# The first two units of a diffusion backbone on scaled, unnormalised x, with the scale groups of the modulation loaded ahead of the shift groups

## The chip, the cores and the metric

The kernel runs on one core of a Trainium2 chip. The metric is the device time of one execution in microseconds (us); lower is better. The engines are TensorE (PE in the profile, with PEld for its weight loads), VectorE (DVE), ScalarE (ACT), GpSimd (POOL) and SyncE (SP), which here only issues transfers. An engine's name with a q (SPq, ACTq) is its queue of issues.

## The reference

Two layers of a diffusion backbone run over 256 latent tokens x and 256 context tokens, each a row of 1024 channels. Each layer has a half-step SwiGLU feed-forward network (FFN), a token mixer and a second FFN. Only the first FFN of the first layer and what it begins with matter here. For each of two streams (tokens modulated by c, context by c_ctx):

```python
m = split(silu(c) @ mod_w[l] + mod_b[l], 9)      # m[0] shift, m[1] scale, m[2] gate of the first FFN
u = rms_norm(x, norm_ffn1[l]) * (1 + m[1]) + m[0]
a, g = split(u @ w_in, 2)
x = x + 0.5 * m[2] * ((silu(g) * a) @ w_out)
```

rms_norm divides each token by the root of its mean square over the 1024 channels (plus 1e-6) and multiplies by a gain per channel. The root is one number per token, so it may be applied behind the matmul: with A = gain * (1 + scale), u @ w is rstd * ((x * A) @ w) + shift @ w.

## The kernel before, in words

**Layout.** Activations lie channels on partitions: `x`, `u_hi` and `u_lo` have 8 chunks (DC) of 128 channels by 512 tokens (256 latent, 256 context). Products keep fp32 precision by splitting both sides in a rounded part and a rest (`w_hi`, `w_lo`, `u_hi`, `u_lo`); `three` (L1112 to L1115) issues three matmuls of 512 columns per chunk. A weight tile is 8 chunks of 128 x 128, 512 KB, in a ring of four. SP loads `w_raw` (L313) once POOL is through with the tile four before; ACT rounds it into `w_hi` (L434), POOL subtracts into `w_lo` (L402), PE may then use it. A hidden unit of the FFN takes two tiles, j = 0 (value) and j = 1 (gate). `pair` (L1117) runs both tiles of a unit chunk by chunk, so that it can follow the making of u; units 0 and 1 go through it, later ones through `products`.

**Modulation.** `mod_w` is read in groups of 512 columns, 2 MB each. Groups 0 and 1 hold the shifts of the first norm, 2 and 3 its scales; within each kind the first group serves chunks 0 to 3 and the second chunks 4 to 7. `mod_rounds` (L1183) runs 16 matmuls for a group into bank 6, ACT copies it (`copy_mod`, L505), `mod_turn` (L1191) transposes it into bank 7, and DVE reduces it into columns (`mod_extract`, L829). Four groups (N_START) are loaded by SP into `mod_first` (L317), in the order of `START_GROUPS`; the later ones come by ACT's queue (`load_mod`, L499), one or two transfers ahead of use.

**The start.** SP issues, in this order: identity, vectors, x, ctx, groups 0 and 2, the two tiles of unit 0, groups 1 and 3, then the tiles of unit 1 and all further ones. PE transposes the token rows chunk by chunk (`turn_x`, L1253), DVE copies each chunk to `x` (L934), ACT squares it (L449) and DVE adds the squares up (L768). PE sums over channels (`mean_square`, L1163), ACT takes the root (L464), DVE the reciprocal and a diagonal matrix (L783, L784), and `spread` (L1170) puts rstd on all partitions of bank 5. After groups 0 and 2 are through, DVE forms `colB` (shift) and `colA` (gain times 1 + scale) for chunks 0 to 3 (`columns_norm`, L747 to L749).

**A norm.** In `norm`, DVE makes `tmp` = x * colA * rstd (L799), ACT `u_hi` = tmp + colB, rounded (L488), DVE `u_lo` the rest (L812), each in two halves by stream. In the start it does chunks 0 to 3, then groups 1 and 3 are taken in (`start_columns(1)`), then chunks 4 to 7. PE has these two groups between its fourth and fifth chunk of unit 0, and group 4 between units 0 and 1.

**Later norms.** For k > 0 the first pair doesn't wait for the norm. ACT's `first_scaled` (L456) and DVE's `first_split` (L775) make u_hi and u_lo of x * colA without rstd and shift; PE's first pair uses them, with `mean_square` and `spread` among its chunks, and follows with 32 matmuls of 4 columns that multiply the weights with the shifts (L1153, L1154, from `shift_split`). ACT and DVE then overwrite u with the normalised one for all other units, and `first_hidden` (L868) applies rstd and shift to unit 0's products. ACT's part of the norm begins with w_hi of the tiles 2 and 3 and has those of 4 and 5 ahead of chunks 5 and 7.

From unit 2 on all runs in a loop (`turns`), the same in every sub-layer. DVE and ACT wait for each other and for PE by semaphores; `link` makes DVE wait for its own instruction.

## Time and profile before

| what | value |
|---|---|
| median of 3 runs | 2162.15 us (2160.63 to 2166.5) |
| the profiled execution, its own time | 2160.53 us |
| its span, first to last instruction | 2158.7 us |
| mean granted clock of TensorE | 0.984 |
| busy: PE / DVE / ACT / POOL | 96% / 39% / 31% / 44% |
| chain that ended last | PE 81%, issue 8%, DVE 5%, POOL 4% |

The page is one profiled execution. A busy share is the time in which an engine has at least one instruction under way; the matmuls are pipelined, so a mean duration of one is longer than the distance to the next. The chain follows the work that ended last back from the end. Time on it is time of the kernel; idle time of an engine off the chain costs nothing. The granted clock is a share of 2.4 GHz, 0.5 being 1.2 GHz. In the timeline an entry gives start, duration, engine, line, operation, out<-in and, in brackets, how long the engine had been idle and who released it.

### The profile page before, as it was taken

The numbers are of one execution on the slowest core, as the hardware profiler recorded it, in microseconds if no ns is written. First come the engines' busy times: TensorE is split into PE (matmuls) and PEld (weight loads), VectorE is DVE, ScalarE is ACT, GpSimd is POOL, SyncE is SP. The second block draws the span as 40 slices with busy tenths as digits, with TensorE's granted clock in tenths as the row PEclk, the third lists the DMA queues.
The fourth block names the chain that finished last, engine by engine and source line by source line (L and its number), as shares of the span: only waits on it lengthen the run. The fifth ranks groups of instructions, "written<-read, shape, count | busy, mean of one in ns | idle before, by whom it ended". The sixth has DMA issues, their size and how long they took to land.

```text
span 2158.7 us, 30089 instructions
## 1 busy us (share of the span) xinstructions
PE 2081.9 (96%) x10694; PEld 1675.0 (78%) x10694; DVE 849.6 (39%) x1320; ACT 670.0 (31%) x1057; POOL 940.7 (44%) x424
## 2 busy tenths in 40 slices
PE   4899999999999999999999999999999899989998
PEld 2677777887557888877877787787778766989998
DVE  4333123356472213623132454322333836573313
ACT  3221222243343223422222242222224333444333
POOL 2244434343102444444444444444434321876886
PEclk8999999999999999999999999999999899999999
DMA  8555654244101333454455236534624420654564
GB/s 280 167 164 154 218 163 150 81 112 105 48 1 49 97 90 95 122 171 143 120 156 169 67 105 202 155 100 138 192 75 112 125 69 16 180 157 137 170 187 127
DMA packets 445425, 278.98 MB, mean 129 GB/s; under 512 B 33906, under 2 KB 407148, under 8 KB 445356
## 3 DMA queue, kind: packets, MB, share of 16 engines
q1 hardware_dynamic: 401868, 206.79, 33.6%
q10 hardware_dynamic: 43360, 71.05, 10.0%
q8 instruction: 42, 0.69, 0.1%
q0 software_dynamic: 128, 0.23, 0.0%
q14 instruction: 27, 0.22, 0.0%
HBM read 276.98 MB, written 1.05 MB: 129 GB/s over the span
## 4 chain that ended last, share of the span: by engine, by line
PE 81%; issue 8%; DVE 5%; POOL 4%; SPq 1%; ACT 1%; DMA 1%; POOLq 0%; DVEq 0%; ACTq 0%
PE bank L1113 24%; PE bank L1115 24%; PE bank L1114 24%; POOL w_lo L402 4%; PE bank L1183 3%; PE bank L1392 1%; PE bank L1340 1%; DVE u_lo L812 1%; PE bank L1376 1%; PE bank L1191 1%; DVE tmp L799 1%; SPq L313 1%; DMA w_raw<-in_ffn_w_in 1%; DVE rstd L971 1%; SPq L317 1%
## 5 line engine op out<-in xcount | busy, mean ns | idle before, releaser
L402 POOL TENSOR_TENSOR w_lo<-w_raw,w_hi 128x1024 fp32r<-128x1024 f32 (+2 forms) x412 | 937.5, 2292 | 1205.4 <-ACT w_hi L434 1205.3
L1113 PE MATMUL bank<-u_hi,w_hi 128*128 128x512 f32 (+1 forms) x2016 | 742.2, 368 | 22.8 <-DVE u_lo L812 20.7
L1114 PE MATMUL bank<-u_lo,w_hi 128*128 128x512 f32 (+1 forms) x2016 | 728.2, 361 | 0.0
L1115 PE MATMUL bank<-u_hi,w_lo 128*128 128x512 f32 (+1 forms) x2016 | 727.6, 361 | 0.0
L1113 PEld LDWEIGHTS bank<-u_hi,w_hi 128*128 128x128 f32 x2016 | 387.5, 192 | 105.0 <-issue 28.0
L434 ACT ACTIVATE w_hi<-w_raw 128x1024 fp32r<-128x1024 f32 (+2 forms) x412 | 385.6, 969 | 177.3 <-PE bank L1115 167.2
L1115 PEld LDWEIGHTS bank<-u_hi,w_lo 128*128 128x128 f32 x2016 | 386.8, 192 | 57.5
L1114 PEld LDWEIGHTS bank<-u_lo,w_hi 128*128 128x128 f32 x2016 | 387.6, 192 | 56.0 <-issue 1.7
L857 DVE TENSOR_TENSOR hf<-bank,sg 128x512 f32<-128x512 f32 (+1 forms) x85 | 53.2, 626 | 586.5 <-ACT sg L529 586.5
L1113 PE MATMUL bank<-h_hi,w_hi 128*128 128x512 f32 (+1 forms) x704 | 258.2, 367 | 3.9 <-DVE x L841 3.2
L1115 PE MATMUL bank<-h_hi,w_lo 128*128 128x512 f32 (+1 forms) x704 | 256.1, 364 | 0.0
L1114 PE MATMUL bank<-h_lo,w_hi 128*128 128x512 f32 (+1 forms) x704 | 254.3, 361 | 0.0
L529 ACT ACTIVATE sg<-bank 128x512 f32<-128x512 f32 (+1 forms) x85 | 46.4, 546 | 655.4 <-PE bank L1115 655.4
L865 DVE TENSOR_TENSOR h_lo<-hf,h_hi 128x512 f32 (+3 forms) x88 | 177.8, 2020 | 9.4
L841 DVE SCALAR_TENSOR_TENSOR x<-bank,colG,x 128x256 f32 (+1 forms) x136 | 60.5, 480 | 279.6 <-PE bank L1115 277.8
L1113 PEld LDWEIGHTS bank<-h_hi,w_hi 128*128 128x128 f32 x704 | 132.3, 188 | 27.9 <-issue 6.3
L1115 PEld LDWEIGHTS bank<-h_hi,w_lo 128*128 128x128 f32 x704 | 132.2, 188 | 23.0
L1114 PEld LDWEIGHTS bank<-h_lo,w_hi 128*128 128x128 f32 x704 | 132.1, 188 | 21.9
L1064 DVE TENSOR_TENSOR tmp<-bank,sig 128x512 f32<-128x512 f32 (+1 forms) x48 | 23.8, 552 | 182.1 <-PE bank L1115 182.1
L449 ACT ACTIVATE sq<-x 128x512 f32<-128x512 f32 (+3 forms) x56 | 32.0, 571 | 194.1 <-DVE x L841 184.2
L687 ACT ACTIVATE sig<-bank 128x512 f32<-128x512 f32 (+1 forms) x48 | 23.7, 493 | 180.2 <-PE bank L1115 180.2
L1183 PE MATMUL bank<-mod_w,sil 128*32 128x512 f32 x512 | 61.6, 598 | 0.0
(146 smaller groups left out, 1667.5 us busy)
## 6 DMA issues: line engine op xcount, KB each, us to landing
w_raw<-in_ffn_w_in SPq DMA_DIRECT2D x176, 512.0 KB, 3.9
mod_w<-in_mod_w ACTq DMA_DIRECT2D x64, 1024.0 KB, 7.3
w_raw<-in_w_in SPq DMA_DIRECT2D x68, 512.0 KB, 3.8
w_raw<-in_ffn_w_out SPq DMA_DIRECT2D x64, 384.0 KB, 3.4
w_raw<-in_ffn_w_out SPq DMA_DIRECT2D x64, 320.0 KB, 3.3
mod_first<-in_mod_w SPq DMA_DIRECT2D x4, 2048.0 KB, 14.9
w_raw<-in_w_o SPq DMA_DIRECT2D x16, 512.0 KB, 4.0
w_raw<-in_w_in SPq DMA_DIRECT2D x16, 256.0 KB, 4.3
```

The source lines that it names most:

```text
L402: pool.tensor_tensor(w_lo[:, slot, 0:n, :], w_raw[:, slot, 0:n, :], w_hi[:, slot, 0:n, :].bitcast(F32), ALU.subtract).then_inc(S("w_lo_rea ...
L434: act.activation(w_hi[:, slot, 0:n, :], w_raw[:, slot, 0:n, :], ACT.Copy).then_inc(S("w_hi_ready"), 1)
L449: act.activation(sq[:, par, 0:n], x[:, bass.ds(m, 1), 0:n].rearrange("p a n -> p (a n)"), ACT.Square).then_inc(S("sq_ready"), 1)
L529: act.activation(sg[:, b, 0:n], bank[:, 2 * b + 1, 0:n], ACT.Silu).then_inc(S("silu_ready"), 1)
L841: last = dve.scalar_tensor_tensor(out=xs, in0=bank[:, b, cols], scalar=colG[:, k, v, bass.ds(m, 1)], in1=xs, op0=ALU.mult, op1=ALU.add)
L857: dve.tensor_tensor(hf[:, b, 0:n], bank[:, 2 * b, 0:n], sg[:, b, 0:n], ALU.mult).then_inc(S("h_prod"), 1)
L865: dve.tensor_tensor(h_lo[:, bass.ds(s, 1), 0:n].rearrange("p a n -> p (a n)"), hf[:, b, 0:n], hs.bitcast(F32), ALU.subtract).then_inc(S("h ...
L1064: last = dve.tensor_tensor(tmp[:, j, 0:n], bank[:, 3 + j, 0:n], sig[:, j, 0:n], ALU.mult)
L1113: pe.matmul(dst, w_hi[:, slot, kk, :], hi_[:, ka, 0:n], start=start, stop=False)
L1114: pe.matmul(dst, w_hi[:, slot, kk, :], lo_[:, ka, 0:n], start=False, stop=False)
L1115: return pe.matmul(dst, w_lo[:, slot, kk, :], hi_[:, ka, 0:n], start=False, stop=stop)
L1183: last = pe.matmul(bank[32 * j:32 * j + 32, 6, :], sil[:, MK * kh + j, :], w[:, j, :], start=kh == 0, stop=kh == 1)
```

## The change

The norm k = 0 is done as the later ones. The scale groups are loaded first: SP's order becomes ident, vectors, x, ctx, group 2, tiles of unit 0, groups 3 and 0, tiles of unit 1, group 1. The squares are taken by ACT from the token rows themselves (four instructions of 1024 columns with an accumulated sum), so that chunk-wise squares, DVE's adds and PE's mean square leave the start; the transposes use banks 3 to 5. `columns_norm` is split in `columns_scale`, `columns_shift` and `split_shift`, each for both streams at once. DVE and ACT make the scaled x for chunks 0 to 3 behind the first group and for 4 to 7 behind the second. PE has the second group's rounds behind chunk 1 and its transposes behind chunk 2, `spread` and the third group at chunks 5 and 6, the fourth at chunk 7; then it waits for `shift_ready`, now behind the chunks for every k, and runs the small matmuls. The shifts of chunks 4 to 7 are made in the middle of DVE's norm. Unit 1 uses the normalised u. Group 4 comes behind unit 1, rounds and transposes together. In the diff "..." stands for lines left out; bookkeeping of semaphore counts is among them.

```diff
-    START_GROUPS = (0, 2, 1, 3)
+    START_GROUPS = (2, 3, 0, 1)
...
-        for G in range(2):
-            load_first(G)
+        def load_start(j, c):
+            col = j * D_FF + c * P
+            load(phases[order[0]], [(0, P, 0, DC, t["ffn1_w_in"][0].rearrange("(k p) c -> p k c", p=P)[:, :, col:col + P])], j, c, 0, 2)
+        load_first(0)
         for j in range(2):
-            load(phases[order[0]], [(0, P, 0, DC, t["ffn1_w_in"][0].rearrange("(k p) c -> p k c", p=P)[:, :, j * D_FF:j * D_FF + P])], j, 0, 0, 2)
-        for G in range(2, N_START):
-            load_first(G)
+            load_start(j, 0)
+        load_first(1)
+        load_first(2)
+        for j in range(2):
+            load_start(j, 1)
+        load_first(3)
...
-                            if ph.g0 == 0 and c == 0 and isinstance(i, int) and i == 0:
+                            if ph.g0 == 0 and isinstance(i, int) and i == 0:
...
         def first_scaled(k, m, i=0):
-            act.wait_ge(S("x_done"), x_count(k) + m + 1 + i * 2)
+            if k:
+                act.wait_ge(S("x_done"), x_count(k) + m + 1 + i * 2)
+            else:
...
-            act.wait_ge(S("ms_ready"), k + 1)
+            act.wait_ge(S("ms_ready"), k)
             act.activation(root[:, 0:n], bank[:, 4, 0:n], ACT.Sqrt, bias=eps_col[:, 0:1]).then_inc(S("root_ready"), 1)
...
-        def norm(k, key=None):
+        def norm(k, key):
             n = norm_tokens(k)
+            ph = phases[key]
             if k:
-                ph = phases[key]
                 root_of(k)
-                for q in (2, 3):
-                    hi(ph, q % ph.nu, q // ph.nu)
+            for q in (2, 3):
+                hi(ph, q % ph.nu, q // ph.nu)
             for d in range(DC):
-                if k == 0 and d == DC // 2:
-                    for G in range(2, N_START):
-                        copy_mod(G)
-                    load_mod(BG_BASE[0, 1], *mod_plan(0, 1, BG_BASE[0, 1]))
-                if k and d in (DC - 3, DC - 1):
+                if d in (DC - 3, DC - 1):
                     q = 4 + (d == DC - 1)
                     hi(ph, q % ph.nu, q // ph.nu)
                 q = DC * k + d
-                if k:
-                    act.wait_ge(S("first_used"), DC * (k - 1) + d + 1)
+                act.wait_ge(S("first_used"), DC * k + d + 1)
                 act.wait_ge(S("t_ready"), q + 1)
                 for v in range(n // SEQ):
                     cols = slice(SEQ * v, SEQ * v + SEQ)
                     last = act.activation(u_hi[:, d, cols], tmp[:, d % 3, cols], ACT.Identity, bias=colB[:, k, v, d:d + 1])
                 last.then_inc(S("u_hi_done"), 1)
-                if k and d == DC - 1:
+                if d == DC - 1:
                     act.wait_ge(S("rstd_spread"), k + 1)
                     act.activation(rstd[:, 0:n], bank[:, 5, 0:n], ACT.Copy).then_inc(S("rstd_copied"), 1)
...
-                        if start and c == 0:
-                            if not k:
-                                for j in range(2):
-                                    hi(ph, j, 2)
-                        elif not start:
+                        if not start:
                             for j in range(2):
                                 hi(ph, j, c + 1, i, 2)
                         if c == 1 and mods and not (start and k):
...
-        for d in range(DC):
-            square_at(d, d, d % 2, d, TOK)
-        root_of(0)
-        for G in range(2):
+        for a in range(2 * TT):
+            act.wait_ge(rows_loaded[a // TT], 16)
+            act.activation(sq[:].rearrange("p a n -> p (a n)"), tok_rows[:, a, :], ACT.Square, accum_out=row_sum[:, a:a + 1])\
+               .then_inc(S("rows_squared"), 1)
+            act.wait_ge(S("rows_squared"), a + 1)
+        act.activation(root[:, 0:2 * TT], row_sum[:], ACT.Sqrt, bias=eps_col[:, 0:1], scale=1.0 / D).then_inc(S("root_ready"), 1)
+        copy_mod(0)
+        first_hi(order[0])
+        for h in range(2):
+            if h:
+                copy_mod(1)
+            for d in range(DC // 2 * h, DC // 2 * h + DC // 2):
+                first_scaled(0, d)
+        for G in range(2, N_START):
             copy_mod(G)
-        first_hi(order[0])
-        for j in range(2):
-            hi(phases[order[0]], j, 1)
-        norm(0)
+        load_mod(BG_BASE[0, 1], *mod_plan(0, 1, BG_BASE[0, 1]))
+        norm(0, order[0])
         for l in range(DEPTH):
             ffn(l, 1)
...
+            split_shift(k)
...
+        def columns_scale(k, d0, d1):
...
-            gain = vec[:, l, V_N1 + DC * w + d0:V_N1 + DC * w + d1]
...
+            a0, a1 = 3 * DC * w + DC + d0, 3 * DC * w + DC + d1
+            both = [P, 2, d1 - d0]
+            gain = vec[:, l, V_N1 + DC * w + d0:V_N1 + DC * w + d1].unsqueeze(1).to_broadcast(both)
+            link(dve.tensor_tensor(colA[:, k, :, d0:d1], modcol[:, l, :, a0:a1], vec[:, l, a0:a1].unsqueeze(1).to_broadcast(both), ALU.add))
+            dve.scalar_tensor_tensor(out=colA[:, k, :, d0:d1], in0=colA[:, k, :, d0:d1], scalar=1.0, in1=gain,
+                                     op0=ALU.add, op1=ALU.mult).then_inc(S("scale_ready"), 1)
+            dve.wait_ge(S("scale_ready"), d1 // (DC // 2) if k == 0 else k + 2)
...
+        def columns_shift(k, d0, d1):
+            l, w = k // 3, k % 3
+            b0, b1 = 3 * DC * w + d0, 3 * DC * w + d1
+            link(dve.tensor_tensor(colB[:, k, :, d0:d1], modcol[:, l, :, b0:b1],
+                                   vec[:, l, b0:b1].unsqueeze(1).to_broadcast([P, 2, d1 - d0]), ALU.add))
+        def split_shift(k):
+            shift = colB[:, k].rearrange("p v d -> p d v")
+            link(dve.tensor_copy(shift_split[:, :, 0:2], shift))
+            dve.tensor_tensor(shift_split[:, :, 2:4], shift, shift_split[:, :, 0:2].bitcast(F32), ALU.subtract)\
+               .then_inc(S("shift_ready"), 1)
         def columns_gate(k):
...
+            if k:
+                rstd_of(k)
+            dve.wait_ge(S("rstd_spread"), k + 1)
             scale(0)
...
                 if halfway:
-                    start_columns(1)
+                    start_shift(1)
+                    split_shift(0)
                     scale(d + 1)
...
-                    if start and k:
+                    if start:
...
         for d in range(DC):
             dve.wait_ge(S("x_turned"), d + 1)
-            dve.tensor_copy(x[:, d, :], bank[:, 4 + d % 3, :]).then_inc(S("x_done"), 1)
-            if d:
-                add_squares(d - 1, (d - 1) % 2, TOK)
-        add_squares(DC - 1, (DC - 1) % 2, TOK)
-        def start_columns(h):
-            for G in range(2 * h, 2 * h + 2):
-                mod_extract(G, 0, START_GROUPS[G])
-            dve.wait_ge(S("mod_kept"), 2 * h + 2)
-            columns_norm(0, DC // 2 * h, DC // 2 * h + DC // 2)
+            dve.tensor_copy(x[:, d, :], bank[:, 3 + d % 3, :]).then_inc(S("x_done"), 1)
+        dve.wait_ge(S("x_done"), DC)
+        def start_scale(h):
+            mod_extract(h, 0, START_GROUPS[h])
+            dve.wait_ge(S("mod_kept"), h + 1)
+            columns_scale(0, DC // 2 * h, DC // 2 * h + DC // 2)
+            for d in range(DC // 2 * h, DC // 2 * h + DC // 2):
+                first_split(0, d)
+        def start_shift(h):
+            mod_extract(2 + h, 0, START_GROUPS[2 + h])
+            dve.wait_ge(S("mod_kept"), 3 + h)
+            columns_shift(0, DC // 2 * h, DC // 2 * h + DC // 2)
         rstd_of(0)
-        start_columns(0)
+        start_scale(0)
+        start_scale(1)
+        start_shift(0)
         norm(0)
...
-            if early:
-                pe.wait_ge(S("shift_ready"), k)
             for kk in range(DC):
                 if early:
-                    pe.wait_ge(S("first_u_ready"), DC * (k - 1) + kk + 1)
+                    pe.wait_ge(S("first_u_ready"), DC * k + kk + 1)
                 else:
                     pe.wait_ge(S("u_ready"), DC * k + kk + 1)
...
-                    if kk == MEAN_AT[n[0]]:
+                    if k and kk == MEAN_AT[n[0]]:
...
-                if first and k == 0 and kk == DC // 2 - 1:
-                    for G in range(2, N_START):
-                        mod_rounds(G)
-                        mod_turn(G)
+                if early and k == 0:
+                    for at, step, G in ((1, mod_rounds, 1), (2, mod_turn, 1), (5, mod_rounds, 2), (6, mod_turn, 2), (7, mod_rounds, 3),
+                                        (7, mod_turn, 3)):
+                        if kk == at:
+                            step(G)
             if early:
+                pe.wait_ge(S("shift_ready"), k + 1)
                 for u, s in enumerate(slots):
...
+                    begins = half == 0 and isinstance(i, int)
                     for c in range(2):
                         hidden(c + i * 2, c, i)
-                        if with_mods:
+                        if with_mods and not begins:
                             (mod_rounds, mod_turn)[c](G)
+                    if with_mods and begins:
+                        pe.wait_ge(S("h_prod"), s0 + 1)
+                        mod_rounds(G)
+                        mod_turn(G)
...
-                last = pe.transpose(bank[:, 4 + d % 3, P * a:P * a + P], tok_rows[:, a, P * d:P * d + P], ident[:])
+                last = pe.transpose(bank[:, 3 + d % 3, P * a:P * a + P], tok_rows[:, a, P * d:P * d + P], ident[:])
...
-        mean_square(0)
-        for G in range(2):
-            mod_rounds(G)
-            mod_turn(G)
-            if G == 0:
-                spread(0)
+        mod_rounds(0)
+        mod_turn(0)
```

## Rows read from the trace of the kernel before

**Rows 1.** The page, busy time of each engine.

```profile
PE 2081.9 (96%) x10694; PEld 1675.0 (78%) x10694; DVE 849.6 (39%) x1320; ACT 670.0 (31%) x1057; POOL 940.7 (44%) x424
```

**Rows 2.** View by stretches, 64 to 480 us: busy time, (instructions), clock, DMA share.

```profile
sum 416.00, PE 416.00 PEld 323.82 DVE 136.89 ACT 110.21 POOL 174.37; mean PE 41.60 PEld 32.38 DVE 13.69 ACT 11.02 POOL 17.44
```

**Rows 3.** Chain of waits, second pair and loop entry: start us, us, what.

```profile
74.26 0.43 PE bank L1113
...
85.41 0.44 PE bank L1191 x4
```

**Rows 4.** Timeline of PE: start us, us, what [idle before].

```profile
12.66 6.12 PE L1253 MATMUL bank<-ident,tok_rows 128*128 128x128 f32 x28 [5.21 <-DMA tok_rows<-in_ctx]
```

**Rows 5.** Timeline, all engines, 31 to 38 us.

```profile
31.36 1.92 PE L1183 MATMUL bank<-mod_first,sil 128*32 128x512 f32 x16
...
33.35 0.60 ACT L505 ACTIVATE mod_part<-bank 128x512 f32<-128x512 f32 x1 [3.49 <-PE bank L1183]
33.85 2.00 ACT L434 ACTIVATE w_hi<-w_raw 128x1024 fp32r<-128x1024 f32 x2
...
34.70 0.19 DVE L829 TENSOR_REDUCE modcol<-bank 128x8 f32<-128x32 f32 x1 [3.03 <-PE bank L1191]
...
34.98 4.64 POOL L402 TENSOR_TENSOR w_lo<-w_raw,w_hi 128x1024 fp32r<-128x1024 f32 x2 [30.80 <-ACT w_hi L434]
35.12 2.22 DVE L748 TENSOR_TENSOR colA<-modcol,vec 128x4 f32<-128x4 f32 x1
37.37 2.27 DVE L749 SCALAR_TENSOR_TENSOR colA<-colA,vec 128x4 f32<-128x4 f32 x1
```

**Rows 6.** Timeline, all engines, 43 to 47 us.

```profile
43.11 2.81 DVE L812 SCALAR_TENSOR_TENSOR u_lo<-tmp,colB,u_hi 128x256 fp32r<-128x256 f32 x2 [1.20 <-ACT u_hi L488]
...
46.06 0.77 PE L1113 MATMUL bank<-u_hi,w_hi 128*128 128x512 f32 x1 [11.40 <-DVE u_lo L812]
```

**Rows 7.** Timeline, all engines, 58 to 64 us.

```profile
58.43 1.00 ACTq L499 DMA_DIRECT2D mod_w<-in_mod_w  x2
...
63.97 0.79 PE L1113 MATMUL bank<-u_hi,w_hi 128*128 128x512 f32 x1 [4.23 <-DVE u_lo L812]
```

**Rows 8.** Chain of waits, SP's issues at the start: start us, us, what.

```profile
2.56 0.49 SPq L317
3.09 6.06 SPq L317
...
14.42 5.29 SPq L313
```

**Rows 9.** DMA issues at 2.56, 3.09, 14.42: count, KB, us to landing.

```profile
mod_first<-in_mod_w SPq DMA_DIRECT2D x1, 2048.0 KB, 15.4
...
mod_first<-in_mod_w SPq DMA_DIRECT2D x1, 2048.0 KB, 20.4
...
w_raw<-in_ffn_w_in SPq DMA_DIRECT2D x1, 512.0 KB, 12.3
```

**Rows 10.** Timeline of DVE in a later norm.

```profile
894.12 0.88 DVE L812 SCALAR_TENSOR_TENSOR u_lo<-tmp,colB,u_hi 128x256 fp32r<-128x256 f32 x2
...
895.70 0.88 DVE L812 SCALAR_TENSOR_TENSOR u_lo<-tmp,colB,u_hi 128x256 fp32r<-128x256 f32 x2
```

**Rows 11.** View by stretches of 2 us; PEclk is the granted clock.

```profile
48.00:50.00 2.00, 2.00 (x8) 1.57 (x7) 1.81 (x5) 0.91 (x2) 0.00 (x0) 0.69 0.31 92
...
68.00:70.00 2.00, 2.00 (x7) 1.56 (x6) 0.13 (x1) 0.00 (x0) 0.00 (x0) 0.57 0.00 0
...
892.00:894.00 2.00, 2.00 (x14) 1.75 (x14) 1.75 (x5) 1.31 (x4) 0.00 (x0) 1.00 0.72 198
```

**Rows 12.** One line's instructions, L1153, 460 to 500 us: ns min/median/max.

```profile
L1153 PE MATMUL bank<-shift_split,w_hi x16: 167/251/251, 470.5 to 473.8; 128*128 128x4 f32 x16
```

**Rows 13.** Timeline of PE, small matmuls near 897 us.

```profile
896.91 0.35 PE L1154 MATMUL bank<-shift_split,w_lo 128*128 128x4 f32 x1
...
897.12 0.35 PE L1153 MATMUL bank<-shift_split,w_hi 128*128 128x4 f32 x1
```

74 lines of the change are left out of this document (34 added, 40 removed).

## The prediction

> **What bounds the kernel now.** I read the page first, then the view by stretches, then the timeline of the start, then the transfers. The page's busy times give the engine: the matmul row is 96% of the span [rows 1]. The view by stretches says where it isn't busy: from 64 to 480 us TensorE (PE) is busy in every microsecond, 416 of 416 [rows 2]. So whatever happens ahead of 64 us reaches the end of the span only through the moment at which PE comes out of the start. I take as that moment the first product of the third hidden unit, at 85.41 + 0.44 = 85.85 us [rows 3]: there the loop body begins in both kernels, and from there the work is the same. The question is when the changed kernel gets there.
>
> The timeline of the start says how the 85.85 arise. PE turns the tokens from 12.66 on, waits from 34.7 to 46.06 for the first normalised chunk, runs four of eight chunks, then two groups of modulation, waits 4.23 us up to 63.97, and runs the other four [rows 4 to 7]. The first wait has two causes that fall together: the modulation groups in front of it, and the locked VectorE (DVE): two instructions on 4 columns each took 2.22 and 2.27 us, each until one of GpSimd's (POOL's) two w_lo subtractions ended [rows 5].
>
> **The change, part by part.** All times are from the span's start.
>
> *Transfers.* Landing is issue [rows 8] plus the time to landing [rows 9]: the first group at 2.56 + 15.4 = 18.0, the next at 3.09 + 20.4 = 23.5, so 5.5 us per group; the second of the two weight tiles behind them at 14.42 + 12.3 = 26.7, so 1.6 us per tile. In the new order (group, two tiles, two groups, two tiles, group): group of the first scales 18.0, tiles 19.6 and 21.2, second scales 26.7, first shifts 32.2, tiles 35.4, last shifts 40.9. SP issues the same bytes, its queue is full in both.
>
> *Token phase.* Eight adds of squares leave DVE, which now only copies; 28 transposes took 6.12 us with DVE in the way at times [rows 4], 0.87 for the four of a chunk; with one of DVE's two instructions per chunk gone I take 0.73, an estimate (at 0.87 it would be 1.1 more): 12.66 + 8 x 0.73 = 18.5. Squares move to ACT on 1024 columns: nearest row is w_hi's, 2.00 for two [rows 5]. Even if all four begin only when both token blocks are there, at 12.66, and take 1.4 each with their waits, they end at 18.3. ACT is wanted next at 20.5, DVE wants the root much later, so I cost this at nothing; with the cover gone (squares twice as long) some 4 us would show. The mean-square matmuls (8) and the spread leave this place too.
>
> *To the first product.* The first group's rounds 1.92 [rows 5]: 18.5 to 20.4. From the end of rounds before (33.28) the timeline runs copy, two w_hi, transposes, reduction, POOL from 34.98 [rows 5]; all of it moved to 20.4, 12.8 earlier: copy 20.5, w_hi 21.1 to 23.1 (tile 1 is there at 21.2), reduction 21.9, POOL 22.2 to 26.8. Between the reduction's end and POOL's start one short instruction fits, as one did before ahead of 35.12; that is the sum of the scales. The gain product waits for the end of POOL's first, 24.5. ACT scales in 0.9 (0.91 for two halves, [rows 11]), then DVE's split of chunk 0 waits for POOL's second, 26.8, and takes 0.9, as two u_lo [rows 10]. **First product at 27.7, 18.4 us earlier than 46.06.**
>
> *First two units.* 48 matmuls. At the upper level of the clock the second pair took 11.15 for 48 [rows 3], 0.43 for the first and 0.228 for each after it; at half that clock twice as much, 0.43. PE started at 46.06 and 63.97 [rows 6, 7]; the granted clock was 0.69 on average from 48 to 50 and 0.57 from 68 to 70 [rows 11], so it rose from 0.5 to 1 at about 49.2 and 69.7, 3.2 and 5.7 us after the start; I take 4.2, ten matmuls at 0.43, and 0.35 of first latency. Chunks 0 and 1: 27.7 to 32.7. Second scales, rounds 1.9: 34.6. Chunk 2: 36.0; transposes 0.45: 36.4; chunk 3: 37.8. Meanwhile reduction, two column sums, 0.9 of ACT and 0.9 of DVE give chunk 4 at 39.1: a wait of 1.3. Chunks 4 and 5: 41.8; spread, four passes of 512 columns by my estimate, 1.0: 42.8; rounds of the first shifts: 44.7; chunk 6, transposes, chunk 7: 47.9; rounds of the last shifts: 49.8; copy and transposes 1.3 (33.35 to 34.70 before): **51.1**. Nothing in here is starved of transfers.
>
> *The wait added.* PE now waits for the split shifts. DVE makes them in the middle of the second normalisation, behind its chunk 3, and ACT does that normalisation behind copy_mod, two DMA issues and two w_hi. The last copy starts at 49.85; issues 1.0 from there [rows 7]; two w_hi 2.0: 52.85; u_hi of chunk 0: 53.75. POOL has w_lo for tiles 2 and 3 from 52.0, 2.3 each. u_lo is two instructions with two SBUF operands. By [rows 5] such a one waits out POOL's running instruction, and the next waits again: 54.3, 0.45, POOL to 57.05, 0.45: 57.5. Chunks 1 and 2 at 1.6 each (1.58 from one u_lo to the next, [rows 10]): 60.7; chunk 3: 61.7; reduction, sum, copy, difference, 0.2 each: **shifts at 62.5**. PE stands still for 11.4 us. The row of [rows 6] (2.81 for two u_lo behind one subtraction) shows the lock on this very instruction. The Trainium skill, page SBUF — State Buffer, section Who interferes with whom, says that a VectorE instruction with two SBUF inputs and a GpSimd one that reads SBUF exclude each other for a whole instruction; the trace's 2.22 and 2.27 agree. Without a lock the shifts would come 2.4 earlier, at 60.1.
>
> *Shift matmuls.* 32 that weren't there for this norm. One later norm has every second of them from 470.5 to 473.8, 0.22 apart, so 0.11 from one to the next [rows 12]. In another they are 0.21 apart at 896.9 [rows 13]; the granted clock was still 1.00 at 892 to 894 [rows 11], so it went to the lower level, 1.2 GHz, while they ran. After 11 us of standing still it is at the lower level: 32 x 0.213 = 6.8: 69.3. Ends: 3.6 and 6.8.
>
> *Second pair.* Weights and u are there (chunk 5's w_hi waits for unit 0's release at 65.9, its u is ready by about 70.5, PE wants it at 78). 10 x 0.43 + 38 x 0.228 + 0.2 = 13.1: 82.4. Before it took 11.15.
>
> *Fourth group.* Its rounds no longer stand between the two pairs but behind the second, followed at once by its transposes: 1.9 + 0.65 of copy that nothing covers + 0.45: **85.4**, against 85.85. ACT's silu of the second unit now stands behind that copy, its w_hi for units ahead start near 86.5; PE has 11 us of work by then, POOL's two end by 93. That hides them.
>
> *Later norms.* columns_norm does both streams in one instruction: 8 instructions become 5, each about as short as the reduction of [rows 5], 0.19. They stand in front of updates that PE seldom waits for. I take 0.2 in all.
>
> Sum: 85.4 - 85.85 - 0.2 = **-0.6 us**. The profiled execution took 2160.53 (span 2158.7, 1.8 around it), 1.6 below the median of 2162.15; so 2159.9 against the profile and 2161.5 against the median. Eighteen microseconds are won at the first product and given back: 11.4 by the wait for shifts, 6.8 by the shift matmuls, the rest by groups that were hidden in front.
>
> About 0.3%, 6.5 us, is what a measurement of this kernel can tell from no change.
>
> **The rivals.**
> *The wait is short (faster).* If POOL doesn't hold u_lo (-2.4), the shift matmuls run at 0.112 (-3.2) and the second pair finds the upper clock (-1.9), the time is 2161.5 - 7.5 = 2154.0. For it: at 470 us they all ran at 0.11. Against: there PE had no pause before them [rows 12]. 17%.
> *Small matmuls bring the clock back.* If they count as work, the clock is up some 4.2 us into them: 20 at 0.213 and 12 at 0.112 make 5.6, and the second pair 11.2: 3.1 less, 2158.4. Against: the clock fell in their midst between 894 and 897 [rows 11, 13]. 10%. The Trainium skill, page TensorE: Matmul & The Clock Gate, Part 1, says of the return that "the HW doesn't count instructions"; by it short ones might do. No row here shows them raising the clock.
> *The clock stays low in the first pair (slower).* Rounds and waits are now strewn among the chunks. If that holds the clock down from 27.7 on through all eight chunks, 38 more matmuls cost 0.2 each, the shifts come that much later, and the time is 2161.5 + 7.6 = 2169.1. Decides from 5 us on, about 33 more matmuls. Against: it rose soon after 46.06 and stayed up over two groups of rounds. 8%.
> *The tiles land with the second group,* 26.7 instead of 21.2, because the rings mix them: w_hi of tile 1 then ends at 27.8, POOL at 30.2, first product 31.1, 3.4 later: 2164.9. For it: the second group was issued at 3.09, with x, ctx and the first still under way [rows 8, 9]. 8%.
> That the first product doesn't move at all (row squares late, first group late) would add about 18: 2180; 2%.
> The forecast itself keeps 55%.
>
> **How the numbers follow.** Its own bounds: clock return 3.2 to 5.7 us twice (1.2 us), transposes 1.1, lock 0 to 2.4, noise of the runs about 2: 2157.5 to 2165.5. The range reaches to the faster rival and to just short of the slower: 2154.5 to 2168. Faster by over 0.3% (below 2155.7): most of the first rival and a tail, 0.2. Slower (above 2168.6): 0.11. Same: 0.69.
>
> **What would show it.** Right: first product of u near 27.7; chunk 4 after a gap of about 1.3; PE's longest wait in the start about 11 us, ended by DVE's shift_split at about 62.5; 32 shift matmuls 0.21 apart; third unit at about 85.4. Two POOL subtractions at 52 to 57 with an u_lo of over 2 us. Wrong: a wait below 6 us, shift matmuls 0.11 apart, the third unit before 80 or after 92, or new waits of PE behind 90.

## The result and the profile after

The changed kernel takes 2169.57 us (median of 8 runs, 2168.0 to 2171.69), the kernel before on the same chip 2166.56 (8 runs, 2160.03 to 2168.22): a ratio of 1.0025, 95% interval 1.0013 to 1.0036. That is 5.4 us slower (2.8 to 7.8), where the prediction had 0.6 us faster and a range that ended at 2168.0. (Here and below the ratio with its interval decides. It is not the quotient of the two medians, which is 1.0014: the single runs of the kernel before spread over 8 us.)

Two lines of the page after: the span (before 2158.7) and PE's row, which answers to [rows 1].

```profile
span 2165.8 us, 30143 instructions
...
PE 2095.6 (97%) x10718; PEld 1680.5 (78%) x10718; DVE 857.9 (40%) x1314; ACT 676.4 (31%) x1075; POOL 937.8 (43%) x424
```

The profiled executions differ by 7.1 us. PE is busy for 13.7 us more, with 24 instructions more. So the start was the first place to look, and it is as it was worked out, within 0.7 us at each step. The timeline of the changed kernel, all engines (start us, us, what; they answer to [rows 3 to 7]):

```profile
19.18 1.92 PE L1223 MATMUL bank<-mod_first,sil 128*32 128x512 f32 x16
...
22.80 4.65 POOL L415 TENSOR_TENSOR w_lo<-w_raw,w_hi 128x1024 fp32r<-128x1024 f32 x2 [18.61 <-ACT w_hi L447]
22.95 2.22 DVE L768 SCALAR_TENSOR_TENSOR colA<-colA,vec 128x8 f32<-128x8 f32 x1
...
28.27 0.77 PE L1153 MATMUL bank<-u_hi,w_hi 128*128 128x512 f32 x1 [5.79 <-DVE u_lo L807]
...
39.56 0.50 PE L1153 MATMUL bank<-u_hi,w_hi 128*128 128x512 f32 x1 [1.23 <-DVE u_lo L807]
...
52.82 4.82 POOL L415 TENSOR_TENSOR w_lo<-w_raw,w_hi 128x1024 fp32r<-128x1024 f32 x2 [25.37 <-ACT w_hi L447]
...
54.52 3.40 DVE L844 SCALAR_TENSOR_TENSOR u_lo<-tmp,colB,u_hi 128x256 fp32r<-128x256 f32 x2 [5.09 <-ACT u_hi L499]
...
62.75 0.18 DVE L783 TENSOR_TENSOR shift_split<-colB,shift_split 128x16 fp32r<-128x16 f32 x1
...
62.98 0.37 PE L1193 MATMUL bank<-shift_split,w_hi 128*128 128x4 f32 x1 [11.05 <-DVE shift_split L783]
...
69.62 0.35 PE L1194 MATMUL bank<-shift_split,w_lo 128*128 128x4 f32 x1
...
85.08 0.66 PE L1231 MATMUL bank<-ident,mod_part 128*128 128x128 f32 x4 [0.72 <-ACT mod_part L516]
...
85.49 0.48 PE L1153 MATMUL bank<-u_hi,w_hi 128*128 128x512 f32 x1
```

The first product comes at 28.27 (before 46.06, [rows 6]), chunk 4 after a gap of 1.23, the wait for the split shifts is 11.05 us, the 32 small matmuls start from 62.98 to 69.62, 0.214 apart, and the third hidden unit begins at 85.49, predicted at 85.4. (The prediction's 85.85 for the kernel before was the end of its transposes, [rows 3]; the product's own row there stands at 85.60. Start against start the changed kernel is 0.11 us earlier in these two traces, and not 0.36, as the expectations below have it.) The view by stretches (stretch, its length, busy time and instructions of PE, PEld, DVE, ACT, POOL, then the granted clock) shows the clock where it answers to [rows 11]: at the lower level at the first products and in the long wait, and back 3 to 4 us after products of 512 columns begin, in both places.

```profile
28.00:30.00 2.00, 1.73 (x4) 1.47 (x5) 2.00 (x6) 0.50 (x2) 0.00 (x0) 0.50 1.04 385
...
32.00:34.00 2.00, 2.00 (x17) 0.94 (x19) 0.00 (x0) 0.00 (x0) 0.00 (x0) 0.98 1.19 300
...
56.00:58.00 2.00, 0.00 (x0) 0.00 (x0) 2.00 (x2) 0.00 (x0) 1.65 (x1) 0.50 1.05 377
...
72.00:74.00 2.00, 2.00 (x8) 1.53 (x8) 2.00 (x2) 1.98 (x4) 1.59 (x1) 0.74 0.69 208
```

So the 7 us arise behind the start, in the part of which the prediction said "from there the work is the same". Comparing the starts of the same matmuls in the two traces, the lag of the changed kernel grows from 0.4 us at 229 to 1.9 at 450, 6.5 at 673, 9.9 at 1655 and ends at 7.4. Most of the step at 673 (4.0 us between 520 and 661) goes with a fall of the granted clock at 575 to 600 (mean 0.80) that the trace before has not, and where the lag shrinks (around 900, 1290 and 1950), the trace before has the longer time at the lower clock. The rest grows where PE reads h, cat or mg (the FFNs' output phases, the gate and output projections) and not in the input phases, which read u. There the same instructions run at another pace. Twenty threes of h (w_hi by h_hi, w_hi by h_lo, w_lo by h_hi, 512 columns each) lie between the two rows of each fence, first before, then after:

```profile
1232.25 0.39 PE L1113 MATMUL bank<-h_hi,w_hi 128*128 128x512 f32 x1
...
1245.98 0.39 PE L1113 MATMUL bank<-h_hi,w_hi 128*128 128x512 f32 x1
```

```profile
1232.13 0.39 PE L1153 MATMUL bank<-h_hi,w_hi 128*128 128x512 f32 x1
...
1246.13 0.39 PE L1153 MATMUL bank<-h_hi,w_hi 128*128 128x512 f32 x1
```

13.73 us before, 14.00 after: 687 ns a three against 700. Over all threes in the trace without a wait in them, from the start of one to the start of the next, the mean is 686.9 and 700.2 for h, 689.1 and 702.1 for cat, 686.8 and 700.1 for mg, and 682.2 and 682.1 for u. With 528, 64 and 64 threes of 512 columns and 304 of 256 columns (6 to 7 ns more each) the sum is 10.8 us.

No instruction of these phases was changed. What was changed is where h, cat and mg lie: the new tile row_sum, 16 bytes per partition, takes 32, and all tiles declared behind it move up: h_hi from byte 144832 of each partition to 144864. u and the weights lie in front of it and didn't move.

### The profile page after: what moved, and what is told of

It reads as the page before. It is cut to its first block, busy times and chain, and to the rows that moved or that the text cites. A ratio compares the mean times of both kernels' runs of the same rounds, so it can differ in the third digit from the quotient of the medians.

```text
span 2165.8 us, 30143 instructions
## 1 busy us (share of the span) xinstructions
PE 2095.6 (97%) x10718; PEld 1680.5 (78%) x10718; DVE 857.9 (40%) x1314; ACT 676.4 (31%) x1075; POOL 937.8 (43%) x424
## 4 chain that ended last, share of the span: by engine, by line
PE 91%; DVE 5%; issue 1%; DMA 1%; ACT 1%; POOL 1%; SPq 0%; DVEq 0%; ACTq 0%; POOLq 0%
PE bank L1153 26%; PE bank L1155 26%; PE bank L1154 26%; PE bank L1223 3%; PE bank L1381 2%; PE bank L1433 2%; PE bank L1417 1%; DVE u_lo L844 1%; PE bank L1231 1%; POOL w_lo L415 1%; DVE rstd L1011 1%; PE bank L1403 0%; DMA tok_rows<-in_ctx 0%; PE bank L1194 0%; DVE smax L1053 0%
## 5 line engine op out<-in xcount | busy, mean ns | idle before, releaser
L1153 PE MATMUL bank<-u_hi,w_hi 128*128 128x512 f32 (+1 forms) x2016 | 740.4, 367 | 14.5 <-DVE u_lo L807 9.1
L1153 PEld LDWEIGHTS bank<-u_hi,w_hi 128*128 128x128 f32 x2016 | 385.8, 191 | 98.3 <-issue 30.7
L1153 PE MATMUL bank<-h_hi,w_hi 128*128 128x512 f32 (+1 forms) x704 | 259.0, 368 | 3.3 <-DVE x L873 3.1
L1155 PE MATMUL bank<-h_hi,w_lo 128*128 128x512 f32 (+1 forms) x704 | 260.6, 370 | 0.0
L1153 PEld LDWEIGHTS bank<-h_hi,w_hi 128*128 128x128 f32 x704 | 133.0, 189 | 31.1 <-issue 6.0
L462 ACT ACTIVATE sq<-x 128x512 f32 (+3 forms) x48 | 26.9, 561 | 185.2 <-DVE x L873 185.2
L844 DVE SCALAR_TENSOR_TENSOR u_lo<-tmp,colB,u_hi 128x256 fp32r<-128x256 f32 x88 | 58.8, 710 | 9.4 <-ACT u_hi L499 9.4
```

The lines of the kernel that those rows point to most:

```text
L844: last = dve.scalar_tensor_tensor(out=u_lo[:, d, cols], in0=tmp[:, d % 3, cols], scalar=colB[:, k, v, d:d + 1], in1=u_hi[:, d, cols].bitca ...
L1153: pe.matmul(dst, w_hi[:, slot, kk, :], hi_[:, ka, 0:n], start=start, stop=False)
L1155: return pe.matmul(dst, w_lo[:, slot, kk, :], hi_[:, ka, 0:n], start=False, stop=stop)
```

## Is it the place or the start?

Both kernels, with nothing but padding or the place of row_sum changed. Four runs on one chip.

```diff
# before_pad32, before_pad64: the kernel before, one unused tile
     rrec = sb("rrec", [P, 2, 2])
+    pad = sb("pad", [P, 4])        # [P, 16] in before_pad64
# after_pad64: the same [P, 4] behind rrec of the changed kernel
# after_home: the changed kernel
-    row_sum = sb("row_sum", [P, 2 * TT])
...
         mod_first = place(st, "mod_first", [P, N_START, DC, MG])
+        row_sum = place(st, "row_sum", [P, 2 * TT])
```

> The kernel before, with one unused tile of 16 bytes per partition placed behind rrec. It issues the same instructions; h, cat and the other tiles behind it move up by 32 bytes per partition, to where the changed kernel has them (h_hi at byte 144864 of each partition in place of 144832). Theory of the place: PE's matmuls that read h, cat and the attention's operands are paced a little slower from such a place, as in the changed kernel, about 14 ns in three matmuls (701 against 687 ns), 8 to 12 us over the whole: a ratio to before of 1.004 to 1.005. Theory of the start (the new instructions at the start, or their effect on the later order of work, cost the time): nothing, 1.000. Theory of the clock (the two kernels differ by where the granted clock falls): nothing that repeats, 1.000 with matmul pace as in before.

Measured: 1.0032 of before (1.0019 to 1.0045), 2170.3 us. Threes of h 700.2 ns, of u 682.1. An unused tile makes the old kernel as slow as the changed one. The theories of the start and of the clock fall as the cause of the loss.

> The changed kernel, with row_sum placed in the room of tok_rows and mod_first, so that h_hi is back at 144832. All instructions are the same. Theory of the place: three matmuls on h in 687 ns again, 8 to 11 us less than the changed kernel, so a ratio to before of 0.999 to 1.000 (the start still reaches the loop 0.36 us earlier). Theory of the start: as the changed kernel, 1.0025 to 1.004. Theory of the clock: 1.000 to 1.003 with the pace of matmuls as in the changed kernel.

Measured: 0.999 (0.9979 to 1.0001), 2164.85 us; h 686.9 ns again. With h at its old place the change is what the prediction said of it: the interval holds the forecast 0.6 us of gain, and no change at all.

> The kernel before, with one unused tile of 64 bytes per partition behind rrec: h_hi at 144896, a multiple of 128 as well as of 64 (144832 is one of 64 alone). Theory of the place, if a multiple of 64 is enough: 1.000, three matmuls in 687 ns. If a multiple of 128 counts: faster than before, three matmuls in 683 or less, up to 3 us. Theories of the start and of the clock: 1.000.

Measured: 1.0044 (1.0031 to 1.0058), 2173.48 us, h 699.8. Neither of the two forms of the theory of the place: 144896 is a multiple of 64 and of 128, and it is slow.

> The changed kernel with one more unused tile of 16 bytes, so that h_hi stands at 144896, a multiple of 128. Theory of the place: as the changed kernel with row_sum elsewhere, 0.998 to 1.000 of before. Theories of the start and of the clock: as the changed kernel, 1.0025 to 1.004.

Measured: 1.0024 (1.0014 to 1.0034), h slow as in before_pad64. So the place matters, but not as alignment to 64 or 128 bytes, which is what I had expected. Before_pad64 shows a sign of what it is: its matmuls alternate between 229 and 238 ns, before_pad32's repeat 231, 231, 238, those of before 229, 232, 226, whatever the other engines do. That looked like PE's own reads falling into step with one another.

## A map of the places

PE alone, the same three matmuls, 16 times at each place:

```
for m0, w0 in places:            # in elements of 4 bytes
    for r in range(16):
        kk = r % 8
        matmul(bank, w_hi[w0 + 128 kk], hi[m0 + 512 kk]); matmul(bank, w_hi[...], lo[...]); matmul(bank, w_lo[...], hi[...])
```

> A kernel of its own that computes nothing of the reference (its output is a constant): PE alone runs the same three matmuls as the FFN's (w_hi with hi, w_hi with lo, w_lo with hi, 128 x 128 by 512 columns), 16 times in a row at each place of the moving operand. Four sections: the moving operands 0 to 2016 bytes, in steps of 32, behind a place that leaves 128 when divided by 512 (as u_hi has it); then the weights moved by 0 to 480 bytes with the moving operands at 0; the same with the moving operands at 320 (where h_hi stands in the kernel before); then the moving operands at 0 to 480 again, with ACT and POOL copying and subtracting beside PE. Theory A (the pace is a matter of the operands' places alone, seen by PE's own reads): three matmuls take 682 ns at offset 0 as for u, 687 at 320, 700 to 701 at 352 and 384, and the rest of the map shows the rule. Theory B (PE's reads collide with those of the other engines or the DMAs, whose tiles did not move with h): one pace at all offsets in the first three sections, and differences in the last alone.

Measured, ns for a three once it has settled (the mean of the fourth to the sixteenth at each place):

| moving operand less weights, bytes modulo 256 | 0 | 32 | 64 | 96 | 128 | 160 | 192 | 224 |
|---|---|---|---|---|---|---|---|---|
| moving operand moved | 680.0 | 700.2 | 686.7 | 700.0 | 699.7 | 702.9 | 699.8 | 699.8 |
| weights moved | 680.6 | 699.4 | 686.6 | 700.2 | 697.6 | 702.9 | 699.8 | 699.7 |

The first line repeats all through 2048 bytes, eight times, within 0.1 ns. With the weights moved instead (section two, and section three with the moving operand at 320) the same figures stand at the same differences, within 3 ns. With ACT and POOL at work beside PE nothing changes; DVE and transfers were not put beside it, but in the whole kernels, where both are at work, the same three paces appear (680.5, 686.9 and 700.2). Theory A holds, its three paces included, and theory B falls: what counts is the moving operand's byte less the weights' byte, modulo 256. Why it is 256, and which part of PE makes it so, no run shows. Rows of the timeline of place_map; ten threes lie between the two of each pair: moving operand at 0, 32 and 64, then weights at 192 (a difference of 64), then both at a difference of 0 with the moving operand at 320 and the weights at 64:

```profile
38.66 0.39 PE L114 MATMUL bank<-mov,w_hi 128*128 128x512 f32 x1
...
45.46 0.39 PE L114 MATMUL bank<-mov,w_hi 128*128 128x512 f32 x1
...
49.62 0.39 PE L114 MATMUL bank<-mov,w_hi 128*128 128x512 f32 x1
...
56.62 0.39 PE L114 MATMUL bank<-mov,w_hi 128*128 128x512 f32 x1
...
60.09 0.39 PE L114 MATMUL bank<-mov,w_hi 128*128 128x512 f32 x1
...
66.96 0.39 PE L114 MATMUL bank<-mov,w_hi 128*128 128x512 f32 x1
...
818.53 0.39 PE L114 MATMUL bank<-mov,w_hi 128*128 128x512 f32 x1
...
825.40 0.39 PE L114 MATMUL bank<-mov,w_hi 128*128 128x512 f32 x1
...
951.96 0.39 PE L114 MATMUL bank<-mov,w_hi 128*128 128x512 f32 x1
...
958.76 0.39 PE L114 MATMUL bank<-mov,w_hi 128*128 128x512 f32 x1
```

6.80, 7.00, 6.87, 6.87 and 6.80 us. The kernels' places fit, as the sizes of the declared tiles give them, each rounded up to 32 bytes: weights at 82048 leave 128 when divided by 256; u leaves 128 (difference 0), h before 192 (64), h after 224 (96), h behind 64 bytes 0 (128). The kernel before had a good place for h by chance, and the best for u.

The map says what to do in the kernel: give h, cat and mg a difference of 0, and it says what 64 bytes in front of the weights would do.

```diff
# before_pad192
     rrec = sb("rrec", [P, 2, 2])
+    pad = sb("pad", [P, 48])
# before_w64
     u_lo = sb("u_lo", [P, DC, TOK], F32R)
+    pad = sb("pad", [P, 16])
     w_raw = sb("w_raw", [P, RING, 8, P])
# after_256: the changed kernel
     rrec = sb("rrec", [P, 2, 2])
+    pad = sb("pad", [P, 40])
```

> The kernel before with an unused tile of 192 bytes per partition behind rrec: h_hi and the other tiles behind it stand 192 bytes higher, at 145024, which leaves 128 when divided by 512, as u_hi and the weights do. Theory A: h, cat and the rest are read at u's pace, three matmuls in 682 to 683 ns against 687, 3 to 4 us less than before: a ratio of 0.998 to 0.999. Theory B (a collision with tiles that did not move): any pace, 687 or 700 as likely, since the distance to those tiles is a new one.

Measured: 0.9981 (0.997 to 0.9992), 2160.53 us; h 680.5 ns. Twenty threes:

```profile
1231.91 0.39 PE L1114 MATMUL bank<-h_hi,w_hi 128*128 128x512 f32 x1
...
1245.51 0.39 PE L1114 MATMUL bank<-h_hi,w_hi 128*128 128x512 f32 x1
```

13.60 us, against 13.73 before. At 256 columns, though, h, cat and mg went from 353 to 360 ns here, so that the threes sum to 2.3 us less and not to the 3 to 4 expected; the measured 4.1 (1.7 to 6.5) holds both.

> The kernel before with 64 unused bytes between u_lo and w_raw: the weights and everything behind them move up by 64 bytes, u_hi and u_lo stay. Theory (only the difference of the two places counts, modulo 256): h less weights is 64 as before, so the three matmuls on h keep 687 ns though h now stands at a multiple of 128; u less weights becomes 192, for which the map has 700 in place of 680: u's three go from 682 to 700, and with some 1400 threes of 512 columns the whole is about 25 us longer, a ratio of 1.010 to 1.014. Rival (h's own place counts): h's three go to 700 as they did at this very place behind 64 bytes of padding, u's stay at 682, and the whole is 7 to 10 us longer.

Measured: 1.008 (1.0056 to 1.0104), 2182.76 us from two runs. Twenty threes of h, then ten of u:

```profile
1232.62 0.39 PE L1114 MATMUL bank<-h_hi,w_hi 128*128 128x512 f32 x1
...
1246.36 0.39 PE L1114 MATMUL bank<-h_hi,w_hi 128*128 128x512 f32 x1
```

```profile
102.96 0.40 PE L1114 MATMUL bank<-u_hi,w_hi 128*128 128x512 f32 x1
...
109.96 0.40 PE L1114 MATMUL bank<-u_hi,w_hi 128*128 128x512 f32 x1
```

h keeps 687 ns at 144896, where it had 700 with the weights at their old place; u takes 700. The rival falls. But the whole came out 17 us longer by the ratio and not 25: the 608 threes of 256 columns of u went from 360 to 340 ns. 24.9 us more for the wide ones and 11.7 less for these leave 13, inside the interval of 12 to 23 us. The map was made at 512 columns, and I had taken it for all widths.

> The changed kernel with 160 unused bytes behind rrec and nothing else, so that h, cat and mg stand at 145024. Against the kernel before with the same places (0.9981 of before): the start, 0.36 us earlier at the loop, and nothing else, so 0.997 to 0.9985 of before. Rival (the later norms or the start's new order cost something of their own): 0.999 to 1.001.

Measured: 0.9973 (0.9962 to 0.9984), 2157.06 us, as forecast; the rival falls. The changed kernel with 160 unused bytes is 0.5% faster than without them (0.9973 over 1.0025, 11.3 us, where the threes' means sum to 13.0).

## The stall of 11 us, taken apart

The prediction laid the wait for the split shifts to DVE's order of work and to POOL holding u_lo. Both with row_sum moved, so that the place plays no part.

```diff
# home_w_early, ACT
+        second_hi(order[0])          # w_hi of tiles 2 and 3
         for G in range(2, N_START):
             copy_mod(G)
# home_shift_early, DVE (and the same lines out of norm's chunk 3)
         start_shift(0)
+        start_shift(1)
+        split_shift(0)
         norm(0)
```

> The changed kernel with row_sum in the room of tok_rows, and with ACT's two w_hi of tiles 2 and 3 made behind chunk 7 of the first scaling in place of at the head of the normalisation; so POOL's two w_lo run at about 43 to 48 in place of 52.8 to 57.6. The shifts stay in the middle of the normalisation. Theory as predicted (4.4 of the 11.1 us for which PE stands are these two w_hi, 2.0, and POOL holding the first u_lo, 2.5): that u_lo takes 0.9 for its two instructions in place of 3.40, the split shifts come at about 58.3 in place of 62.75, PE waits about 6.7 us for them, and the time is 4 to 4.5 us less than with row_sum moved alone. Rival (the long u_lo is no lock but a late u_hi or port traffic of the transfers): it stays above 2 us, and 2 us at most are gained.

Measured: 0.9981 (0.997 to 0.9992), 2160.2 us. That is 4.6 less than after_home's median, but only 2 less by the two ratios, which come from different chips; in the two traces the third unit begins 4.75 us earlier. Its timeline:

```profile
41.83 4.71 POOL L415 TENSOR_TENSOR w_lo<-w_raw,w_hi 128x1024 fp32r<-128x1024 f32 x2 [14.47 <-ACT w_hi L447]
...
52.58 0.88 DVE L850 SCALAR_TENSOR_TENSOR u_lo<-tmp,colB,u_hi 128x256 fp32r<-128x256 f32 x2 [3.25 <-ACT u_hi L504]
...
58.27 0.18 DVE L789 TENSOR_TENSOR shift_split<-colB,shift_split 128x16 fp32r<-128x16 f32 x1
...
58.51 0.37 PE L1199 MATMUL bank<-shift_split,w_hi 128*128 128x4 f32 x1 [6.68 <-DVE shift_split L789]
...
81.48 0.48 PE L1159 MATMUL bank<-u_hi,w_hi 128*128 128x512 f32 x1
```

The first u_lo takes 0.88 for its two instructions where POOL isn't reading, against 3.40 above. The splits come at 58.27 + 0.18, the wait is 6.68, the loop begins at 81.48. The lock (DVE's instruction waits until POOL's is through) is shown on this instruction; it and the two w_hi in front are 4.4 of the 11.

> The changed kernel with row_sum in the room of tok_rows (h at its old place) and with the last shift columns and their split made before the first normalisation's second half in place of behind its chunk 3. Theory of the start as predicted (the stall of 11 us is DVE's order of work, and POOL's two subtractions then hold u_lo): PE waits under 2 us for the split shifts, the shift matmuls begin at about 52 us in place of 62.98, the second pair is paced by u_lo, the first product of the third unit comes at 75 to 79 in place of 85.5, and the whole is 7 to 10 us shorter than with row_sum moved alone: 2155 to 2158. Rival (the shifts were not what PE lacked: u and w_lo of the second pair come too late anyway): the wait only moves to the second pair's first product, and the loop is entered at 83 or later, less than 2 us gained.

Measured: 0.9957 (0.9942 to 0.9972), 2155.82 us, 9.0 less than after_home by the medians and 7 by the ratios. Its timeline:

```profile
53.75 0.18 DVE L783 TENSOR_TENSOR shift_split<-colB,shift_split 128x16 fp32r<-128x16 f32 x1
...
53.90 4.86 POOL L415 TENSOR_TENSOR w_lo<-w_raw,w_hi 128x1024 fp32r<-128x1024 f32 x2 [26.28 <-ACT w_hi L447]
...
53.98 0.27 PE L1190 MATMUL bank<-shift_split,w_hi 128*128 128x4 f32 x1 [0.97 <-DVE shift_split L783]
...
55.74 3.29 DVE L843 SCALAR_TENSOR_TENSOR u_lo<-tmp,colB,u_hi 128x256 fp32r<-128x256 f32 x2 [0.25 <-ACT u_hi L499]
...
60.15 0.77 PE L1150 MATMUL bank<-u_hi,w_hi 128*128 128x512 f32 x1
...
78.05 0.48 PE L1150 MATMUL bank<-u_hi,w_hi 128*128 128x512 f32 x1
```

The wait is 0.97 us and the loop begins at 78.05. POOL still holds the first u_lo for 3.29 us, but now PE has the shift matmuls to run meanwhile. They run 0.11 apart for seven of them, and then 0.21: the clock falls in them though the pause right in front of them is under 1 us (PE was busy for 2.3 of the 4 us from 50 to 54).

Both cures together, the shifts early and h at a difference of 0:

> The changed kernel with both cures: the last shift columns and the split made ahead of the normalisation, and 160 unused bytes behind rrec, so that h, cat and mg stand at 145024, which leaves 128 when divided by 256 as the weights do. Theory (the pace is set by the moving operand's place less the weights' place, modulo 256 bytes; the start by DVE's order): three matmuls in 682 ns on h, entry of the loop at about 77.5, 4 to 5 us less than with the shifts early and h at 144832: about 2151.5 us, a ratio to before of 0.993 to 0.995. Rival (gains in pace are given back by more drops of the granted clock): the pace shows, the time stays at 2155 to 2157.

Measured: 0.9919 (0.9902 to 0.9935), 2148.08 us, h 680.4 ns, the loop entered at 75.58. It beats both kernels, and the forecast by 3.4 us; the rival falls. It enters the loop 2.5 us ahead of home_shift_early, the place having no part in that: its first product comes 1.2 us earlier, and 24 of its shift matmuls run 0.11 apart before the clock falls, against seven above, which is worth 1.7.

## Other widths

```diff
# narrow_192, on early_256: at_of(n) is 48 for 256 columns, else 0
-                    hs = h_hi[:, bass.ds(s, 1), 0:n]...
+                    hs = h_hi[:, bass.ds(s, 1), at_of(n):at_of(n) + n]...
# the same for h_lo, cat, mg, the last FFN's u, and in three() for what PE reads
```

> A kernel of its own that computes nothing of the reference (its output is a constant), PE alone, three matmuls 16 times at each place as in the first map. Four sections: 256 columns at offsets 0 to 480 in steps of 32; 512 columns at offsets 0 to 64 in steps of 4 bytes; 384 columns at 0 to 224; 128 columns at 0 to 224. Theory (the rule of 256 bytes is one of the places, and its costs hang on the number of columns): 256 columns give 360 ns at 0, 362 at 32, 353 at 64, 340 at 192 and the same again 256 bytes higher; places that are no multiple of 32 are among the slow ones at 512 columns (700). Rival (the 340 came from the weights' own place at 82112): 192 gives 353 to 362 as well.

Measured, ns for a three:

| difference | 0 | 32 | 64 | 96 | 128 | 160 | 192 | 224 |
|---|---|---|---|---|---|---|---|---|
| 384 columns | 520.0 | 520.0 | 520.0 | 530.0 | 527.8 | 520.0 | 523.9 | 520.0 |
| 256 columns | 360.0 | 353.3 | 353.3 | 360.0 | 356.0 | 356.2 | 353.3 | 355.4 |
| 128 columns | 335.0 | 335.2 | 335.0 | 335.0 | 335.0 | 335.0 | 335.0 | 335.0 |

256 columns repeat after 256 bytes too. At 512 columns steps of 4 bytes give anything from 680.0 (at 0) over 686.2 (at 28 and 60) to 719.1 (at 20), so the expected "slow unless a multiple of 32" is wrong. And 192 gives 353.3 at 256 columns, not 340: neither the theory nor the rival as I had put them.

> The kernel with both cures (shifts early, h at 145024), in which the operands that are read with 256 columns (u of the last FFN, h of the last FFN, cat and mg of the second layer) are written and read 48 columns, 192 bytes, further along their rows of 512. Theory: 656 threes of 256 columns take 340 ns in place of 360: 13 us less than that kernel's 2148.1, so about 2135, a ratio to before of 0.986 to 0.988; the 236 threes of u in the second layer's head and gate stay at 360. Rival (340 came from the weights' own place): 2148 again.

Measured: 0.9882 (0.9866 to 0.9899), 2140.73 us, 7.4 less than early_256 where 13 were expected: the rival falls, and the theory's size is wrong. cat and mg reach 340, u and h of the last FFN only 353 to 355. Ten threes of mg in early_256, then in narrow_192:

```profile
1905.39 0.28 PE L1151 MATMUL bank<-mg_hi,w_hi 128*128 128x256 f32 x1
...
1908.99 0.28 PE L1151 MATMUL bank<-mg_hi,w_hi 128*128 128x256 f32 x1
```

```profile
1903.92 0.28 PE L1164 MATMUL bank<-mg_hi,w_hi 128*128 128x256 f32 x1
...
1907.32 0.28 PE L1164 MATMUL bank<-mg_hi,w_hi 128*128 128x256 f32 x1
```

3.60 and 3.40 us. By the medians, 128 x 20 ns and 528 x 7 ns are 6.3 us of the 7.4. So at 256 columns and a difference of 192 there are two paces, 340 and 353, and which one a loop settles to I can't say: nothing was tried that tells it apart. It is no matter of 192 alone: at a difference of 64 mg has 353 in all 48 threes without a wait in the trace before, but 340 in 27 of 51 in home_shift_early's; and u of the last FFN, at 192 in both, has 340 in before_w64 and 353 here.

## Why the prediction was wrong

- *First product at 27.7:* 28.27; the transposes took 0.80 a chunk where 0.73 was the estimate, and the rounds began at 19.18 and not 18.5. Of the locked DVE instructions of [rows 5] one is left, 2.22 us. *Gap at chunk 4, 1.3:* 1.23. *Shifts at 62.5:* 62.75. *Shift matmuls 0.213 apart:* so. *Loop at 85.4:* 85.49. All steps of the start held. The one reason that was off: I put the lower clock in the shift matmuls down to the 11 us of standing still. In home_shift_early there was no such pause, and it fell as well. The trace of before has it without any pause: there the clock fell at 895.7, 2.5 us into the shift matmuls of [rows 13], with PE busy in every microsecond from 888 on.
- *"There the loop body begins in both kernels, and from there the work is the same"* is the step that failed. The instructions are the same, but a new tile of 16 bytes moved the operands of 656 threes of 512 columns by 32 bytes, from a difference of 64 to the weights, where a three takes 687 ns, to one of 96, where it takes 700: 10.8 us by the threes' means. The sum had no term for the tile, though the changed kernel declares it. Nor could the signs of being wrong show it, since a slower pace is no new wait behind 90 us.
- *The profiled execution as the yardstick:* it was, it seems, a lucky one in its start. In it PE waited 11.40 us for the first product [rows 6] and the loop began at 85.60. The four padded copies of the same start waited 12.7 each and entered at 88.4 to 89.6. The traces show where 1.3 us of that come from. Before:

```profile
39.67 0.16 DVE L747 TENSOR_TENSOR colB<-modcol,vec 128x4 f32<-128x4 f32 x1
...
40.59 4.65 POOL L402 TENSOR_TENSOR w_lo<-w_raw,w_hi 128x1024 fp32r<-128x1024 f32 x2 [0.97 <-ACT w_hi L434]
```

  and before_pad192:

```profile
37.62 9.23 POOL L403 TENSOR_TENSOR w_lo<-w_raw,w_hi 128x1024 fp32r<-128x1024 f32 x4 [33.45 <-ACT w_hi L435]
...
42.32 2.26 DVE L748 TENSOR_TENSOR colB<-modcol,vec 128x4 f32<-128x4 f32 x1
...
44.62 2.26 DVE L749 TENSOR_TENSOR colA<-modcol,vec 128x4 f32<-128x4 f32 x1
...
49.98 0.77 PE L1114 MATMUL bank<-u_hi,w_hi 128*128 128x512 f32 x1 [12.68 <-DVE u_lo L813]
```

  In the trace of before POOL was through with unit 0's tiles before unit 1's was ready, and in its pause of 0.97 us DVE's next three instructions ran unlocked, 0.16 us each. In the padded four POOL went on without a pause (9.2 us for four), and four DVE instructions were locked, not two; only the first u_lo was then free of it. No second trace of the unpadded kernel was kept, so that its trace was the exception and not the padding is inferred. The changed start entered at 85.3 to 86.8 in four traces. What the start is worth on average is best read from the four pairs with h at the same place, by their ratios: 2.2 us (after_home and before), 1.5 (the changed kernel and before_pad32), 4.3 (the two with 64 bytes) and 1.7 (after_256 and before_pad192), each known to 2 to 4 us; so about 2 us, and not 0.4 or less.
- *The level:* the changed kernel's median lies 8.1 us above the forecast 2161.5, but 4.4 of these are the kernel before itself, 2166.56 in eight runs against 2162.15 in the three that the prediction had.
- *Sum:* 10.8 for the place less 2.4 for the start makes 8.4, against a measured 5.4 (2.8 to 7.8) and 7.1 in the spans. What is left is of the size of the clock: by its record the lower level was granted for 41 us behind the start in the trace of before and 44 in that after, but for 31 to 55 us over all kernels here, half of it lost. The single runs of one kernel spread over 1 to 14 us, and they do so with the clock: after_home's six runs at a granted clock of 0.979 to 0.981 took 2164.9 to 2165.9 us, its five at 0.983 and 0.984 2159.6 to 2162.4. Between kernels it fits too: before_pad64 had before's clock (0.982 on average), and its threes sum to 9.2 us where 9.5 were measured; before_pad32 had 0.9845, and of its 10.8 us only 6.9 were measured. What makes the clock fall more often in one run than in the next, no run shows.
- *Rivals:* none of them was the case. The nearest in time, the clock staying low in the first pair (2169.1), is refuted by the clock's row at 32 to 34 us, 0.98; that its time is right to 0.5 us is luck. The wait was not short, no small matmul ran at 0.11 behind it, and the first product came at 28.27 and not at 31.1.

## What to carry to other kernels

A new tile is a part of a change even if nothing on the critical path reads it: list which tiles it moves, and put small tiles behind the large ones or in room that is free anyway. Where PE is busy all the time, compare the start-to-start time of the same matmul in both traces before looking for waits; a few ns in each show in no wait and in no share of busy time. And before a start is redone for the first product's sake, follow DVE's order to the last thing that PE needs: making one split earlier was worth 7 to 9 us, the whole change of order about 2. Last, one trace of a start is one sample: which instruction meets another engine's lock can differ from run to run.

## What the runs showed of the hardware that I had not expected

- Three matmuls of 128 x 128 by 512 columns, the weights reloaded for each, take 680 to 703 ns at multiples of 32 bytes, by the byte place of the moving operand less that of the weights, modulo 256: best at 0, next at 64 (1% more), 2.9 to 3.4% more at the others. At steps of 4 bytes it is 680 to 719 (20). ACT and POOL at work beside it change nothing.
- The order is another at other widths: at 256 columns 0 and 96 are the slowest (360 ns), and 64 and 192 give 340 or 353; at 384 columns 96 is (530 against 520); at 128 columns the place doesn't matter (335).
- The starts of successive matmuls settle into a short pattern of distances (229, 238 ns in turn in before_pad64; 231, 231, 238 in before_pad32) that repeats for hundreds of them.
- A tile of 16 bytes takes 32 of each partition: one and two of them in front of h give the paces of differences 96 and 128 (700.2 and 699.7 ns).
